# Scores of the two later layers as one fp32r product over 96 stacked rows, with q turned inside the Fourier part

## The chip, the cores and the metric

The program runs on one core of one Trainium2 chip. The time is device microseconds of one execution, as the median of several runs. The engines are named as in the profile: PE is TensorE (PEld its weight loads), DVE is VectorE, ACT is ScalarE, POOL is GpSimd and SP is SyncE, which issues the DMAs.

## What is computed

The reference runs a first block (sparse attention, retention, a gated branch mix and a feed-forward part) and then a second block of two layers on x of 256 tokens by 1024 features. The change touches the second block alone, in both layers, and there the attention's scores:

```
u = rmsnorm(x) @ w_in[l]                 # q, k, v (512 wide each), glu_in, four_in
q = apply_partial_rope(rmsnorm(q, qnorm_g[l]), cos, sin)      # 8 heads x 2 halves x 32
k = apply_partial_rope(rmsnorm(k, knorm_g[l]), cos, sin)
sc = einsum('bqhcd,bkhcd->bhcqk', q, k) * 32 ** -0.5          # two score maps a head
p = softmax(sc);  w = p[:, :, 0] - lam * p[:, :, 1];  att = w @ v
g = ga * sigmoid(gb); cv = depthwise conv of g over 31 taps   # branch b
fr = real(fft2(four_in groups))                               # branch c
x = x + (gates of att, cv, fr branches) @ w_out[l];  x = x + feed-forward(x)
```

## The kernel before

All arithmetic is in 32 bits. A large product is made of three fp32r products: a value is split into an upper part (a copy rounded to fp32r) and a lower part (value less upper part), and upper by upper, lower by upper and upper by lower are added in PSUM. The weights come from memory in 207 chunks of at most 128 x 2048, in the order in which they are used. For every chunk SP issues a load into one of four `raw` buffers (`load_raw`, line 400), ACT writes the upper part `whi` (line 917), and DVE and POOL share the lower part `wlo` (lines 1572 and 1352). SP loads chunk i only when both parts of chunk i - 4 are written (lines 402 and 403), and its queue is strictly in order.

A later layer starts with v, four gated units (glu), then k (`k{l}`), q (`q{l}`) and the Fourier input (`xf{l}`), each as two chunks. `qk_out` normalizes and rotates q and k on DVE, ACT and POOL into `qn`. PE turns them (`qk_turned`, line 796, four 128 x 128 transposes for each half of the tokens) into PSUM, and ACT copies them out as `k2T` and `q2T` in f32 (line 1235). A bank of PSUM that held a turned tile is free for the next use when its last reader has signalled.

Then three stages run as one sequence, `weave(chain(fourier(), attention(), after_attention()), back, 4)`. `back` holds the products of twelve gate units (`g{l}_f`, one chunk and 48 products each) and of the first output projection. `fourier` has five steps with nothing between them. `attention` has 20 steps, with four eighths of a gate unit (24 products) between two of them, so that one chunk is used in two steps. Step u works like this, with u = 2 * head + half of the tokens, for u below 16:

- PE: the two score products of step u (line 861, `scores2`), after the turned weights `W2T` of u - 2 and, in even steps, the product with v.
- DVE: `combine(u - 1)` (reciprocal, factor, one tap of the convolution, then `W2`, line 2078), one tap, then the maximum over the scores of u (line 2100), two taps. The 31-tap convolution is 124 DVE instructions (line 2024) that `conv_some` spreads over the stages, until none is left.
- ACT: the two exponentials `E2` of u (line 1297), every second step a gate's output (line 1250), and after the odd steps the next chunk's `whi`.

DVE has a fixed order too: in the rows of q two taps at each of eight points, in those of xf three, six in each Fourier step. `lower` (line 1605) is the subtraction that makes a lower part, `upper` (line 966) the ACT copy that makes an upper part.

Of the kernel before, what the change touches and what calls it, by code (L numbers as in the profile page):

```python
# [92 lines left out]
for _name, _w in SMALL:  # L93
# [6 lines left out]
    "pool_lo", "pool_small", "d_raw0", "d_raw1", "d_raw2", "d_raw3", "d_x0", "d_x1", "d_small", "d_small2", "d_gain",  # L100
    "d_dec", "d_ctab", "d_gnw", "d_gf", "d_cs", "d_cd", "d_out",
)
# [163 lines left out]
def place(nc, ctx):  # L266
# [79 lines left out]
    z = p + 48  # L346
    t.q2T = at("q2T", z, [128, 4, S])
    t.k2T = at("k2T", z + 4, [128, 4, S])
    t.v2 = [at(f"v2{i}", z + 8 + 2 * i, [128, 512]) for i in range(2)]
# [41 lines left out]
def sp_program(sp, t, ev, d):  # L391
# [5 lines left out]
    def load(sem, dst, src, *names):  # L397
        sp.op.dma_start(dst, src).then_inc(*at(sem, *names, by=16))
# [14 lines left out]
    for i in range(len(PLAN)):  # L413
# [19 lines left out]
        for l in range(2):  # L433
            if i == UNITS[f"k{l}"][0] + 2:
                sp.wait_ge(*on("v ends", l, "pe"))
                sp.wait_ge(*on("v ends", l, "dve"))
                load("d_cs", t.csT[:, :, :], d["in_cs"], ("cs", l))
                load("d_cd", t.cdT[:, :, :], d["in_cd"], ("cd", l))
        load_raw(i)
    for tt in range(2):  # L440
# [6 lines left out]
def pe_program(pe, t, ev, pb):  # L447
# [340 lines left out]
    def layer(l, norm):  # L788
# [13 lines left out]
        run(rows(f"xf{l}", *h))  # L802
        qk_turned("q")
        ev.name("pe_turned", ("projected", l, "pe"))

        def fourier():
            for g in range(5):
                if g < 4:
                    for tt in range(2):
# [18 lines left out]
        def attention():  # L828
            yield
            for u in range(20):  # L830
# [22 lines left out]
                if u < 16:  # L853
                    hd, tt = u // 2, u % 2
                    rg = slice((hd % 4) * 32, (hd % 4) * 32 + 32)
                    for w in "qk":
                        for half_ in range(2):
                            pe.wait_ge(*on("free", (w, l, "T", half_)))
                    pe.wait_ge(*on("E2", l, u - 2) if u >= 2 else on("T12", l, 2 + u))
                    for c in range(2):  # L860
                        product(t.sc[u % 2][:, c * S:c * S + S], t.q2T[rg, c * 2 + hd // 4, tok(tt)],
                                t.k2T[rg, c * 2 + hd // 4, :], names=[("scores2", l, u)] * c)
                yield
# [35 lines left out]
def act_program(act, t, ev, pb):  # L899
# [308 lines left out]
    def layer(l, norm):  # L1208
# [24 lines left out]
        def qk_turned(w):  # L1233
            for tt in range(2):
                turned_out((w, l, "T", tt), (t.q2T if w == "q" else t.k2T)[:, :, tok(tt)])

# [4 lines left out]
                                     [("k", l, "T", tt) for tt in range(2)])))  # L1241
        qk_turned("q")
        done = []

        def gate_out(f):
            def out(p):
                name = (f"g{l}_{f}", 0)
                act.wait_ge(*on("got", *name))
                for v in range(2):
                    act.op.activation(t.gm2[:, 2 * f + v, :], bank(name)[:, v * S:v * S + S],  # L1250
# [15 lines left out]
        def fourier():  # L1266
            for g in range(5):
                if g < 4:
                    act.wait_ge(*on("fourier 1", l, g))
# [278 lines left out]
def dve_program(dve, t, ev, pb):  # L1548
# [438 lines left out]
    def layer(l, norm):  # L1987
# [59 lines left out]
        for w in "kq":  # L2047
            for _ in rows(f"{w}{l}", qk_out(w)):
                conv_some(2)
        for _ in rows(f"xf{l}", value_out(f"xf{l}", t.xf[0][:, :], [("k", l, "T", tt) for tt in range(2)])):  # L2050
            conv_some(3)

        def fourier():
            for g in range(5):
                if g >= 1:
                    k = g - 1
                    lower([("fr", l, k)], t.frl[:, k, :], t.ob[:, 0:256], t.frh[:, k, :], ("fr hi", l, k))
                conv_some(6)
                yield 0
# [225 lines left out]
```

## Time and profile before

| what | value |
|---|---|
| median of three runs | 1472.41 us (1471.64 to 1473.39) |
| the profiled execution | 1471.79 us, span 1470.5 us |
| mean granted TensorE clock | 0.971 |
| PE busy | 1363.5 us, 93% of the span |
| DVE, POOL, ACT busy | 903.7, 733.3, 653.8 us |
| Fourier part and attention of layer 0 | about 585 to 704 us from the span's start |
| the same of layer 1 | about 1066 to 1186 us |

The span starts with the first instruction and ends with the last; 1.3 us of the profiled execution's own time lie around it. The busy share of PE is a mean over stages that have different limits. Times in the rows further down are microseconds from the span's start, and durations without a unit are in microseconds.

### The profile page before, as it was taken

The numbers are of one execution on the slowest core, as the hardware profiler recorded it, in microseconds if no ns is written. First come the engines' busy times: TensorE is split into PE (matmuls) and PEld (weight loads), VectorE is DVE, ScalarE is ACT, GpSimd is POOL, SyncE is SP. The second block draws the span as 40 slices with busy tenths as digits, with TensorE's granted clock in tenths as the row PEclk, the third lists the DMA queues.
The fourth block names the chain that finished last, engine by engine and source line by source line (L and its number), as shares of the span: only waits on it lengthen the run. The fifth ranks groups of instructions, "written<-read, shape, count | busy, mean of one in ns | idle before, by whom it ended". The sixth has DMA issues, their size and how long they took to land. (4 is left out here: it accounts for less than half of the span.)

```text
span 1470.5 us, 21695 instructions
## 1 busy us (share of the span) xinstructions
PE 1363.5 (93%) x8946; PEld 1230.8 (84%) x8946; DVE 903.7 (61%) x1155; ACT 653.8 (44%) x884; POOL 733.3 (50%) x325
## 2 busy tenths in 40 slices
PE   6999999989989898799988999999878999899999
PEld 4878899889978696578987999879657899699987
DVE  5554465467773559976565656445997646556542
ACT  4634435355553443345644444335334464444432
POOL 3653254655554359333665445445833356445453
PEclk9999999999999999999998999999898999899999
DMA  7653224444444452222444455546322234355551
GB/s 276 244 193 144 86 102 172 172 173 172 172 172 172 157 217 88 89 94 104 144 143 158 174 189 182 194 163 219 115 86 87 90 140 147 142 189 182 176 197 58
DMA packets 32786, 227.04 MB, mean 154 GB/s; under 512 B 3632, under 2 KB 4016, under 8 KB 6448
## 3 DMA queue, kind: packets, MB, share of 16 engines
q1 hardware_dynamic: 32688, 225.66, 42.9%
q8 instruction: 71, 1.16, 0.3%
q14 instruction: 27, 0.22, 0.0%
HBM read 224.60 MB, written 1.05 MB: 153 GB/s over the span
## 5 line engine op out<-in xcount | busy, mean ns | idle before, releaser
L1352 POOL TENSOR_TENSOR wlo<-raw,whi 128x416 fp32r<-128x416 f32 (+5 forms) x207 | 604.4, 2923 | 641.2 <-ACT whi L917 543.2
L1572 DVE TENSOR_TENSOR wlo<-raw,whi 128x1632 fp32r<-128x1632 f32 (+5 forms) x207 | 354.5, 1713 | 327.7 <-ACT whi L917 262.2
L519 PE MATMUL ps<-hhi,whi 128*128 128x256 f32 x1696 | 494.5, 292 | 2.6 <-DVE hlo L1605 2.4
L520 PE MATMUL ps<-hlo,whi 128*128 128x256 f32 x1696 | 487.2, 287 | 0.0
L521 PE MATMUL ps<-hhi,wlo 128*128 128x256 f32 x1696 | 486.8, 287 | 0.0
L917 ACT ACTIVATE whi<-raw 128x2048 fp32r<-128x2048 f32 (+1 forms) x207 | 392.6, 1901 | 179.2 <-PE ps L466 153.7
L519 PEld LDWEIGHTS ps<-hhi,whi 128*128 128x128 f32 x1696 | 331.6, 196 | 16.1 <-issue 15.6
L520 PEld LDWEIGHTS ps<-hlo,whi 128*128 128x128 f32 x1696 | 332.0, 196 | 0.4 <-issue 0.2
L521 PEld LDWEIGHTS ps<-hhi,wlo 128*128 128x128 f32 x1696 | 331.7, 196 | 0.0
L2024 DVE SCALAR_TENSOR_TENSOR cv<-gp,sm,cv 128x256 f32<-128x256 f32 x240 | 149.2, 671 | 0.0
L464 PE MATMUL ps<-whi,hhi 128*128 128x512 f32 (+1 forms) x272 | 111.4, 410 | 12.9 <-DVE hlo L1605 5.7
L464 PE MATMUL ps<-whi,ghi 128*128 128x512 f32 x264 | 104.1, 394 | 6.7 <-DVE fu L1951 6.6
L465 PE MATMUL ps<-wlo,hhi 128*128 128x512 f32 (+1 forms) x272 | 107.6, 396 | 0.0
L466 PE MATMUL ps<-whi,hlo 128*128 128x512 f32 (+1 forms) x272 | 107.4, 395 | 0.0
L465 PE MATMUL ps<-wlo,ghi 128*128 128x512 f32 x264 | 103.5, 392 | 0.0
L466 PE MATMUL ps<-whi,glo 128*128 128x512 f32 x264 | 103.5, 392 | 0.0
L1605 DVE TENSOR_TENSOR glo<-fg,ghi 128x256 fp32r<-128x256 f32 x66 | 81.5, 1234 | 2.4 <-ACT ghi L966 2.4
L1171 ACT ACTIVATE fs<-ps 128x256 f32<-128x256 f32 x44 | 16.9, 384 | 147.6 <-PE ps L521 147.6
L1297 ACT ACTIVATE E<-ps,st 128x256 f32<-128x256 f32 x64 | 29.7, 469 | 102.2 <-DVE st L2100 102.2
L464 PEld LDWEIGHTS ps<-whi,hhi 128*128 128x128 f32 x272 | 53.3, 196 | 26.0 <-issue 10.3
L1384 POOL TENSOR_TENSOR st<-st,sm 128x1 f32<-128x1 f32 (+2 forms) x30 | 47.0, 1565 | 50.6 <-DVE st L1624 40.1
L464 PEld LDWEIGHTS ps<-whi,ghi 128*128 128x128 f32 x264 | 50.1, 190 | 17.9 <-DVE fu L1951 7.5
(263 smaller groups left out, 1853.4 us busy)
## 6 DMA issues: line engine op xcount, KB each, us to landing
raw<-in_w SPq DMA_DIRECT2D x205, 1024.0 KB, 4.8
gain<-in_rows SPq DMA_DIRECT2D x6, 512.0 KB, 4.5
raw<-in_w SPq DMA_DIRECT2D x2, 560.0 KB, 5.6
x<-in_x SPq DMA_DIRECT2D x2, 512.0 KB, 6.7
csT<-in_cs SPq DMA_DIRECT2D x2, 512.0 KB, 5.8
out<-x SPq DMA_DIRECT2D x2, 512.0 KB, 2.6
dec<-in_dec SPq DMA_DIRECT2D x1, 768.0 KB, 7.9
sm<-in_small SPq DMA_DIRECT2D x1, 764.0 KB, 15.2
```

The lines of the kernel that those rows point to most:

```text
L464: pe.op.matmul(o, sh, mh, start=start, stop=False, skip_group_check=True)
L465: pe.op.matmul(o, sh, ml, start=False, stop=False, skip_group_check=True)
L466: signalled(pe.op.matmul(o, sl, mh, start=False, stop=stop, skip_group_check=True), names)
L519: pe.op.matmul(o, wh[:, k, c:c + 128], hi[:, k, :], start=first, stop=False, skip_group_check=True)
L520: pe.op.matmul(o, wh[:, k, c:c + 128], lo[:, k, :], start=False, stop=False, skip_group_check=True)
L521: ins = pe.op.matmul(o, wl[:, k, c:c + 128], hi[:, k, :], start=False, stop=last, skip_group_check=True)
L917: act.op.activation(t.whi[i % NHL][:, 0:n], t.raw[i % NRAW][:, 0:n], ACT.Copy).then_inc(*at("act_hi", ("hi", i)))
L1352: pool.op.tensor_tensor(t.wlo[i % NHL][:, c], t.raw[i % NRAW][:, c], t.whi[i % NHL][:, c].bitcast(F32), ALU.subtract).then_inc(*at("pool_l ...
L1384: pool.op.tensor_tensor(o, a, small(t, "mhalf")[:, 0:a.shape[-1]], ALU.pow).then_inc(*at("pool_small", name))
L1572: dve.op.tensor_tensor(t.wlo[i % NHL][:, c], t.raw[i % NRAW][:, c], t.whi[i % NHL][:, c].bitcast(F32), ALU.subtract).then_inc(*at("dve_lo" ...
L1605: dve.op.tensor_tensor(dst, src, hi.bitcast(F32), ALU.subtract).then_inc(*at(sem, *names))
L2024: ins = dve.op.scalar_tensor_tensor(t.cv[:, f, :], t.gp[:, f, j:j + S], cw[:, f, j:j + 1], t.cv[:, f, :], ALU.mult, ALU.add)
```

## The change

The score products of the two later layers are no longer f32 products over 32 rows. k and q are split into upper and lower parts (`kh`, `kl`, `qh`, `ql`). DMAs inside SBUF stack them over 96 partitions: `kst` holds kh, kh, kl, and `qst` holds qh, ql, qh, so that one fp32r product over 96 rows gives the three partial products at once. `qst` has room for four of the eight heads (c * 2 + g for g = 0 or 1); the second group is stacked when the scores of step 7 are done, into the same buffer. A stack is made by 12 DMAs, each from 32 partitions to 32 partitions: 128 KB each for k, 64 KB each for a group of q. All are issued by SP, at a fixed place among the chunk loads. q is turned in the third Fourier step instead of before the first. On DVE, `qk_lower` makes the lower parts, that of k behind the rows of q, with three taps of the convolution drawn ahead of it.

```
@@ sp_program, before load_raw(i)
+            stacked = UNITS[f"xf{l}"][0]
+            if i == stacked + 5:
+                for tt in range(2):
+                    sp.wait_ge(*on("free", ("k", l, "T", tt)))
+                for r, src in enumerate((t.kh, t.kh, t.kl)):
+                    for b in range(4):
+                        load("d_stack", t.kst[32 * r:32 * r + 32, b, :, :].bitcast(F32),
+                             src[32 * b:32 * b + 32, :, :].bitcast(F32),
+                             *([("k stack", l)] * (r + b == 5)))
+            for g, first in enumerate((stacked + 7, stacked + 13)):
+                if i == first:
+                    sp.wait_ge(*on("k stack", l) if g == 0 else on("scores2", l, 7))
+                    for tt in range(2):
+                        sp.wait_ge(*on("free", ("q", l, "T", tt)))
+                    for r, src in enumerate((t.qh, t.ql, t.qh)):
+                        for b in range(4):
+                            load("d_stack", t.qst[32 * r:32 * r + 32, b, :, :].bitcast(F32),
+                                 src[32 * b:32 * b + 32, g:4:2, :].bitcast(F32),
+                                 *([("q stack", l, g)] * (r + b == 5)))
@@ pe_program, layer
         qk_turned("k")
         run(rows(f"xf{l}", *h))
-        qk_turned("q")
@@ fourier, on PE and on ACT
             for g in range(5):
+                if g == 2:
+                    qk_turned("q")
@@ attention, on PE
-                    rg = slice((hd % 4) * 32, (hd % 4) * 32 + 32)
-                    for w in "qk":
-                        for half_ in range(2):
-                            pe.wait_ge(*on("free", (w, l, "T", half_)))
+                    pe.wait_ge(*on("k stack", l))
+                    pe.wait_ge(*on("q stack", l, hd // 4))
...
-                        product(t.sc[u % 2][:, c * S:c * S + S], t.q2T[rg, c * 2 + hd // 4, tok(tt)],
-                                t.k2T[rg, c * 2 + hd // 4, :], names=[("scores2", l, u)] * c)
+                        product(t.sc[u % 2][:, c * S:c * S + S], t.qst[0:96, hd % 4, c, tok(tt)],
+                                t.kst[0:96, hd % 4, c * 2 + hd // 4, :], names=[("scores2", l, u)] * c)
@@ act_program, layer (and gate units 4 to 7 wait for the second q stack)
-                turned_out((w, l, "T", tt), (t.q2T if w == "q" else t.k2T)[:, :, tok(tt)])
+                name = (w, l, "T", tt)
+                upper(("T hi", w, l, tt), (t.qh if w == "q" else t.kh)[:, :, tok(tt)],
+                      bank(name)[:, :].rearrange("p (k s) -> p k s", k=4), name)
@@ dve_program, layer
+        conv_some(3)
+        qk_lower("k")
         for _ in rows(f"xf{l}", ...):
             conv_some(3)
@@ fourier, on DVE
                     k = g - 1
+                    if k == 2:
+                        qk_lower("q")
                     lower([("fr", l, k)], t.frl[:, k, :], t.ob[:, 0:256], t.frh[:, k, :], ("fr hi", l, k))
```

On SP in layer 0, where the chunks of the gate units are loaded, this stands in a row before (one chunk a row, a buffer's number behind raw):

```order
L398 DMA raw_49<-in_w 128x2048 [waits pool_lo,dve_lo]
L398 DMA raw_50<-in_w 128x2048 [waits pool_lo,dve_lo]
L398 DMA raw_51<-in_w 128x2048 [waits pool_lo,dve_lo]
L398 DMA raw_52<-in_w 128x2048 [waits pool_lo,dve_lo]
L398 DMA raw_49<-in_w 128x2048 [waits pool_lo,dve_lo]
L398 DMA raw_50<-in_w 128x2048 [waits pool_lo,dve_lo]
```

and this now, from the second load ahead of the second q stack to the load behind it:

```order
L401 DMA raw_51<-in_w 128x2048 [waits pool_lo,dve_lo]
L401 DMA raw_52<-in_w 128x2048 [waits pool_lo,dve_lo]
L401 DMA qst<-qh 32x2x256 [waits pe_small]
L401 DMA qst<-qh 32x2x256 x3
L401 DMA qst<-ql 32x2x256 x4
L401 DMA qst<-qh 32x2x256 x4
L401 DMA raw_49<-in_w 128x2048 [waits pool_lo,dve_lo]
```

The twelve stacking DMAs of the second group stand right behind the load of chunk xf + 12, which waits for both lower parts of chunk xf + 8.

On DVE in layer 0, from the end of q's rows to the first Fourier lower part, before:

```order
L2043 TENSOR_SCALAR st<-st 128x16 [waits dve_small]
L2024 SCALAR_TENSOR_TENSOR cv<-gp,sm,cv 128x256 x2
L1572 TENSOR_TENSOR wlo_57<-raw_50,whi_54 128x608 [waits pe_weights,act_hi,d_raw1]
L2024 SCALAR_TENSOR_TENSOR cv<-gp,sm,cv 128x256 x2
L2024 SCALAR_TENSOR_TENSOR cv<-gp,sm,cv 128x256 [waits dve_small] x10
L1572 TENSOR_TENSOR wlo_58<-raw_51,whi_55 128x608 [waits pe_weights,act_hi,d_raw2]
L2024 SCALAR_TENSOR_TENSOR cv<-gp,sm,cv 128x256 [waits dve_small] x3
L1610 COPY xf_146<-ps 128x512 [waits pe_turned,pe_weights]
L2024 SCALAR_TENSOR_TENSOR cv<-gp,sm,cv 128x256 [waits dve_small] x15
L1605 TENSOR_TENSOR frl<-ps,frh 128x256 [waits act_small]
```

and now:

```order
L2068 TENSOR_SCALAR st<-st 128x16 [waits dve_small]
L2049 SCALAR_TENSOR_TENSOR cv<-gp,sm,cv 128x256 x4
L2049 SCALAR_TENSOR_TENSOR cv<-gp,sm,cv 128x256 [waits dve_small]
L1630 TENSOR_TENSOR kl<-ps,kh 128x4x128 [waits act_small] x2
L1597 TENSOR_TENSOR wlo_57<-raw_50,whi_54 128x608 [waits pe_weights,act_hi,d_raw1]
L2049 SCALAR_TENSOR_TENSOR cv<-gp,sm,cv 128x256 [waits dve_small] x12
L1597 TENSOR_TENSOR wlo_58<-raw_51,whi_55 128x608 [waits pe_weights,act_hi,d_raw2]
L2049 SCALAR_TENSOR_TENSOR cv<-gp,sm,cv 128x256 [waits dve_small] x3
L1635 COPY xf_150<-ps 128x512 [waits pe_turned,pe_weights]
L2049 SCALAR_TENSOR_TENSOR cv<-gp,sm,cv 128x256 [waits dve_small] x15
L1630 TENSOR_TENSOR frl<-ps,frh 128x256 [waits act_small]
```

Three taps and two subtractions of 128 x 512 now stand ahead of the copy of xf, which the first Fourier product waits for.

On PE in layer 0, the Fourier part now has q's eight transposes behind its first product with `cdT`; before, they stood ahead of the first product with `csT`:

```order
L491 MATMUL ps<-T_152,cdT 128x256 [waits d_cd,act_out]
L491 MATMUL ps<-T_152,cdT 128x256
L499 MATMUL ps<-sm,qn_145 128x128 [waits pool_small]
L499 MATMUL ps<-sm,qn_145 128x128 x3
L499 MATMUL ps<-sm,qn_146 128x128 [waits pool_small]
L499 MATMUL ps<-sm,qn_146 128x128 x3
L491 MATMUL ps<-csT,xf_150 128x512
```

## Rows read from the trace of the kernel before

**Rows 1.** The page, busy time, share of the span and instructions of each engine.

```profile
PE 1363.5 (93%) x8946; PEld 1230.8 (84%) x8946; DVE 903.7 (61%) x1155; ACT 653.8 (44%) x884; POOL 733.3 (50%) x325
```

**Rows 2.** Waits, 585 to 730 us: who waited for whom, total, times, longest.

```profile
ACT E L1297 <- DVE st L2100: 50.8, 16, 5.7
...
PE ps L838 <- DVE W L2078: 11.7, 7, 3.9
...
PE ps L469 <- DVE frl L1605: 5.9, 2, 4.9
```

**Rows 3.** DVE in order of time: start, duration, instruction [idle before].

```profile
631.36 0.79 DVE L1572 TENSOR_TENSOR wlo<-raw,whi 128x608 fp32r<-128x608 f32 x1 [2.15 <-issue]
...
632.45 3.09 DVE L2024 SCALAR_TENSOR_TENSOR cv<-gp,sm,cv 128x256 f32<-128x256 f32 x1
...
639.60 0.69 DVE L2100 TENSOR_REDUCE st<-ps 128x2 f32<-128x512 f32 x1
...
643.23 0.79 DVE L1572 TENSOR_TENSOR wlo<-raw,whi 128x608 fp32r<-128x608 f32 x1 [2.15 <-issue]
```

**Rows 4.** ACT in order of time, the end of the same round.

```profile
640.32 0.47 ACT L1297 ACTIVATE E<-ps,st 128x256 f32<-128x256 f32 x1 [1.11 <-DVE st L2100]
...
641.23 1.90 ACT L917 ACTIVATE whi<-raw 128x2048 fp32r<-128x2048 f32 x1
```

**Rows 5.** PE in order of time: scores, gate products, turned weights.

```profile
607.47 1.13 PE L469 MATMUL ps<-k2T,q2T 32*128 32x256 f32 x4
...
608.75 0.28 PE L520 MATMUL ps<-hlo,whi 128*128 128x256 f32 x1
608.87 0.28 PE L521 MATMUL ps<-hhi,wlo 128*128 128x256 f32 x1
...
647.89 0.44 PE L838 MATMUL ps<-sm,W 128*128 128x128 f32 x2 [1.41 <-DVE W L2078]
...
653.45 1.13 PE L469 MATMUL ps<-k2T,q2T 32*128 32x256 f32 x4
```

**Rows 6.** POOL in order of time: lower parts at the Fourier part and attention.

```profile
584.66 6.61 POOL L1352 TENSOR_TENSOR wlo<-raw,whi 128x1440 fp32r<-128x1440 f32 x2
...
655.16 3.87 POOL L1352 TENSOR_TENSOR wlo<-raw,whi 128x1440 fp32r<-128x1440 f32 x1 [8.01 <-ACT whi L917]
```

**Rows 7.** DVE in order of time, from xf's copy to the Fourier part.

```profile
584.31 0.68 DVE L1610 COPY xf<-ps 128x512 f32<-128x512 f32 x1
584.91 3.28 DVE L2024 SCALAR_TENSOR_TENSOR cv<-gp,sm,cv 128x256 f32<-128x256 f32 x1
...
596.96 2.45 DVE L2024 SCALAR_TENSOR_TENSOR cv<-gp,sm,cv 128x256 f32<-128x256 f32 x6
```

**Rows 8.** DVE, groups by line and form over the span: busy, mean ns.

```profile
L1605 DVE TENSOR_TENSOR hlo<-ps,hhi 128x512 fp32r<-128x512 f32 x24 | 15.9, 688 | 8.4 <-ACT hhi L966 8.3
```

**Rows 9.** SP's queue in order of time: start, time at the issue, what is issued.

```profile
522.14 0.38 SPq L398 DMA_DIRECT2D csT<-in_cs  x1
522.58 0.42 SPq L398 DMA_DIRECT2D cdT<-in_cd  x1
...
659.12 0.33 SPq L398 DMA_DIRECT2D raw<-in_w  x1
```

**Rows 10.** The page, DMA issues: KB each, median us from issue to landing.

```profile
raw<-in_w SPq DMA_DIRECT2D x205, 1024.0 KB, 4.8
...
out<-x SPq DMA_DIRECT2D x2, 512.0 KB, 2.6
```

**Rows 11.** DVE's maxima of steps 0, 8 and 9.

```profile
612.56 0.68 DVE L2100 TENSOR_REDUCE st<-ps 128x2 f32<-128x512 f32 x1
...
660.03 0.68 DVE L2100 TENSOR_REDUCE st<-ps 128x2 f32<-128x512 f32 x1
...
663.38 0.68 DVE L2100 TENSOR_REDUCE st<-ps 128x2 f32<-128x512 f32 x1
```

**Rows 12.** Busy time in one stretch: PE, PEld, DVE, ACT, POOL, granted clock, DMA.

```profile
624.50:631.50 7.00, 7.00 (x29) 6.16 (x29) 4.52 (x12) 5.05 (x12) 0.10 (x1) 0.51 0.37 142
```

More of the change, by code:

```diff
@@ L100 @@
     "pool_lo", "pool_small", "d_raw0", "d_raw1", "d_raw2", "d_raw3", "d_x0", "d_x1", "d_small", "d_small2", "d_gain",
-    "d_dec", "d_ctab", "d_gnw", "d_gf", "d_cs", "d_cd", "d_out",
+    "d_dec", "d_ctab", "d_gnw", "d_gf", "d_cs", "d_cd",
+    "d_stack", "d_out",
 )
@@ L346, in place @@
     z = p + 48
-    t.q2T = at("q2T", z, [128, 4, S])
-    t.k2T = at("k2T", z + 4, [128, 4, S])
+    t.kh, t.kl = (at(n, z + a, [128, 4, S], R32) for n, a in (("kh", 0), ("kl", 4)))
+    t.qh, t.ql = (at(n, p + a, [128, 4, S], R32) for n, a in (("qh", 32), ("ql", 36)))
+    t.kst = at("kst", p, [128, 4, 4, S], R32)
+    t.qst = at("qst", z, [128, 4, 2, S], R32)
     t.v2 = [at(f"v2{i}", z + 8 + 2 * i, [128, 512]) for i in range(2)]
@@ L802, in layer @@
         run(rows(f"xf{l}", *h))
-        qk_turned("q")
-        ev.name("pe_turned", ("projected", l, "pe"))
         def fourier():
             for g in range(5):
+                if g == 2:
+                    qk_turned("q")
                 if g < 4:
@@ L1241, in layer @@
                                      [("k", l, "T", tt) for tt in range(2)])))
-        qk_turned("q")
         done = []
@@ L1248, in out @@
                 act.wait_ge(*on("got", *name))
+                if 4 <= f < 8:
+                    act.wait_ge(*on("q stack", l, 1))
                 for v in range(2):
@@ L1267, in fourier @@
             for g in range(5):
+                if g == 2:
+                    qk_turned("q")
                 if g < 4:
@@ L2049, in layer, with qk_lower @@
                 conv_some(2)
+        def qk_lower(w):
+            for tt in range(2):
+                name = (w, l, "T", tt)
+                hi, lo = (t.qh, t.ql) if w == "q" else (t.kh, t.kl)
+                lower([("free", name)], lo[:, :, tok(tt)], bank(name)[:, :].rearrange("p (k s) -> p k s", k=4),
+                      hi[:, :, tok(tt)], ("T hi", w, l, tt))
+        conv_some(3)
+        qk_lower("k")
         for _ in rows(f"xf{l}", value_out(f"xf{l}", t.xf[0][:, :], [("k", l, "T", tt) for tt in range(2)])):
```

## The prediction

> **What bounds the kernel now.** The page's busy times come first: PE is busy for 1363.5 us, 93% of the span [rows 1]. Read alone, that says that any PE work taken out is time won. The share is a mean, though, so I went to the stretch that the change touches, the Fourier part and the attention of a later layer (585 to 704 us in layer 0; layer 1 repeats it), and asked who waits for whom. PE waits for DVE's `W2` seven times there, 11.7 us in total and 3.9 us at the longest, and 5.9 us for the Fourier lower parts; ACT waits for DVE's maxima in all 16 steps, 50.8 us [rows 2]. So PE is not the engine that sets the pace.
>
> Next, what does? I followed one round of two steps in DVE's order of time. DVE's share of a chunk's lower part starts at 631.36, the next chunk's at 643.23 [rows 3]: a round is 11.87 us. Its links are: DVE's lower part and two small instructions; one tap of the convolution that takes 3.09 us, where six of them take 2.45 us elsewhere [rows 3, 7]; `W2`, tap, maximum; ACT's exponentials; DVE's combine and the odd step's maximum at 639.60 [rows 3]; ACT's exponentials from 640.32; ACT's `whi` of the next chunk at 641.23 for 1.90 us [rows 4]; and at 643.23 DVE again. No link is a PE instruction. PE comes in only if scores are late for a maximum, and they aren't: the scores of step 8 stand from 653.45 [rows 5], their maximum is taken at 660.03 [rows 11].
>
> The long tap lies within a POOL lower part like that of 3.87 us [rows 6]: the tap reads two tensors in SBUF. The Trainium skill has a rule for it (SBUF — State Buffer, "SBUF: two separate sides"): a DVE instruction with two SBUF inputs and a GpSimd instruction exclude each other for a whole instruction. By that rule the new lower parts, which read PSUM and one SBUF tile, would not be held; only the taps ahead of them would be, and by that rule the sum below is as it stands.
>
> **What the change takes off PE.** A step's two score products are four instructions now, 1.13 us from 607.47 [rows 5]. As two fp32r products at the pitch of the gate products (0.12 us from 608.75 to 608.87, same row) they take about 0.3 us. That is 0.8 us a step, 13 us a layer, 26 us in all. I book it at zero: in steps 0 to 15 PE would reach the turning of `W2` 0.8 us sooner and wait 0.8 us longer, since `W2` comes out of a round that has no PE in it (PE's wait of 1.41 us at 647.89 [rows 5] becomes about 3). The cover is gone only if a round gets shorter than PE's own work in it, and nothing in the change shortens it. From the last `W2` on PE sets the end, but there are no scores left there.
>
> **What it adds on DVE ahead of the first scores.** Two k and two q lower parts of 128 x 512, 0.69 us each by the same instruction from PSUM [rows 8], 2.8 us; and three taps drawn ahead (0.41 us each, 2.45 / 6 [rows 7]), 1.2 us that attention gets back later. DVE has no idle time to hide them between q and the attention. Placed on the trace: k's part and the three taps put xf's copy, at 584.31 [rows 7], behind the start of POOL's pair of lower parts (584.66 to 591.27 [rows 6]). The taps ahead of the copy are then held as the one at 584.91 was (3.28 us [rows 7]), twice. I put the copy at 591.5, and the first Fourier product with it, 6 us later than now. Of this DVE's own line only loses about 2.2 us (the 2.5 us of work less an idle of 0.6 us), since the 15 taps behind the copy no longer meet POOL; but PE has then stood for 7 us and restarts at half clock (the granted clock was 0.51 at 624.50 to 631.50, after PE's wait of 3.9 us [rows 2, 12]), and the Fourier steps, a relay of PE, ACT and DVE, lose another 0.8 us by it. q's lower parts, in the fourth step, would end at about 606.5.
>
> Then comes the first q stack: 12 DMAs, one issue after the other. Consecutive issues stand 0.44 us apart (522.14 and 522.58 [rows 9]), so 5.3 us for twelve. The nearest landing is 2.6 us for 512 KB; a load of 1 MB takes 4.8 us [rows 10]. I take 2.6 for the last 64 KB. The scores of step 0 can start at 614.4, and their maximum stands at about 615.5 where it is at 612.56 now [rows 11]: 3 us late. PE has waited for the stack too; its next 24 gate products run at half clock (5 us for 2.9), so step 1's scores come another 1 us late. **Sum: 4 us a layer.** Bounds: 2.5 us, if DVE's 2.8 us less its idle time is all; 7 us, if the landing is 4.8 us and the half clock lasts through. k's stack is covered: it can start when k's lower parts are done, about 578, and has 36 us. q's eight transposes move into PE's wait for the Fourier lower parts.
>
> **What it adds on SP: the second q stack.** Its 12 DMAs stand right behind the load of chunk xf + 12, which waits for POOL's lower part of chunk xf + 8. That part starts at 655.16 and takes 3.87 us [rows 6]; the load goes out at 659.12 [rows 9], though step 7's scores follow the turning at 647.89 [rows 5], some 10 us before. Step 8 needs this stack. From 659.12: the load's own issue 0.4 us, twelve issues of 0.44 us, landing 2.6 us: 667.4. Scores 0.4 us, maximum at 667.9 instead of 660.03 [rows 11], 7.9 us late. Queued behind the waiting scores on PE are 24 gate products, the turning of step 7's `W2` and the scores of step 9. PE has stood for more than 10 us, so these run at half clock: 5.1 us for the 24, and step 9's maximum comes some 6 us behind step 8's, where it is 3.35 us now (660.03 and 663.38 [rows 11]); 2.7 us more. **Sum: 10.6 us a layer.** Bounds: 6.5 us (issues 0.33 us apart, as the busy time of one is, landing 2.6 us, half of the clock loss); 13.5 us (landing as a 1 MB load's, 4.8 us, and all of it).
>
> The Trainium skill speaks against this form of transfer (DMA: Bandwidth & Descriptors, "Rules for kernel authors"): many small transfers should be coalesced, under 64 KB they are mostly overhead. It gives about 2.0 us of fixed cost for a DMA on another queue; with it in place of the landing of 2.6 us each stack would be 0.5 us sooner.
>
> **What it adds later.** After the last `W2` PE runs without waits, and a PE that stood longer before it may restart at half clock: 0 to 2 us, I take 0.5. ACT's copies only change their form, and its new wait for the second stack comes eight steps after the stack. The waits of SP delay loads that are used 12 us later or more.
>
> **Sum.** 4 + 10.6 + 0.5 = 15 us a layer, 30 us in two. The profiled execution took 1471.8 us, 0.6 us under the median of the three runs. 1471.8 + 30 = 1502 us.
>
> **Rivals.**
> 1. PE is the bound after all, and its 26 us come back: 1446 us. For it: 93% busy. Against it: the W2 waits, and a round without PE. It decides if the score products stood between a maximum and the `W2` before it; it would show as rounds of less than 11.87 us. With the additions of the first part it would still be some 1455 us. Chance 6%.
> 2. The second stack is hidden or nearly so, and only the lead-in costs: 8 to 12 us, 1482 us. It asks that the stack goes out some 8 us before POOL's lower part ends, or that twelve issues and the landing take under 2 us. Against it: the order on SP. Chance 10%.
> 3. The DMAs within SBUF are slower than loads: each reads 32 partitions and writes 32, and no DMA in the trace does that. If they take 1 us each one after the other, each stack is 6 to 7 us later: 13 us more a layer, 1528 us. Chance 13%.
> 4. Everything cancels within 0.2% (about 3 us): 3%, as a meeting of 1 and 3.
>
> The forecast, both terms within their bounds, has 68%. Its bounds are 9 x 2 = 18 us and 22.5 x 2 = 45 us, 1490 to 1517 us. To hold the time 8 times in 10 I widen it to 1486 to 1520 us, into the near parts of rivals 2 and 3. Faster by over 0.2% (what a measurement of this kernel can tell from no change): 6%. Within: 3%. Slower: 91%.
>
> **What would show it.** On PE, a wait for the stack DMAs ahead of step 0's scores and one of about 10 us or more ahead of step 8's, in both layers, with a granted clock near 0.5 behind it. On DVE, maxima of steps 0, 8 and 9 late by about 3, 12 and 15 us in layer 0, and rounds of 11.9 us in between, unchanged. PE busy down by 20 us or so, W2 waits up. On SP, the twelve issues 0.44 us apart, right behind a load. The prediction is wrong in its base if the rounds get shorter, and in its size if the last small DMA lands much later or sooner than 2.6 us after its issue.

## The result, and the profile after

| | before | after |
|---|---|---|
| time, us, median (lowest to highest) | 1472.9 (1471.6 to 1477.4) | 1512.0 (1507.8 to 1513.7) |
| profiled execution, us | 1471.8 | 1507.8 |
| ratio, 95% interval | | 1.0256 [1.0225, 1.0286] |

The change makes the kernel 39 us slower. The forecast was 1502 us in a range of 1486 to 1520: the sign and the main mechanism held, and 9 of the 39 us were missing. The profiled execution is the fastest of after, 4 us under the median, so 36 of the 39 us (1507.8 less 1471.8) can be found in the trace.

The page, busy time, share of the span and instructions of each engine, answering to [rows 1]:

```profile
PE 1345.3 (89%) x8882; PEld 1227.9 (82%) x8882; DVE 910.5 (60%) x1163; ACT 654.5 (43%) x884; POOL 729.3 (48%) x325
```

PE does 18 us less and DVE 7 us more. Who waited for whom (total, times, longest) from 570 to 760 us, answering to [rows 2]:

```profile
ACT E L1322 <- DVE st L2136: 58.0, 14, 15.1
...
PE ps L491 <- DMA qst<-qh: 19.5, 2, 14.5
PE ps L860 <- DVE W L2114: 16.7, 7, 4.0
```

PE's waits for `W2` went up from 11.7 (the same from 570 to 760 us) to 16.7 us, and two waits for the q stack are new, 4.9 and 14.5 us. PE in order of time, at the scores of steps 0 and 8 and behind the latter [rows 5]:

```profile
615.83 0.77 PE L491 MATMUL ps<-kst,qst 96*128 96x256 f32 x2 [4.91 <-DMA qst<-qh]
...
673.89 0.80 PE L491 MATMUL ps<-kst,qst 96*128 96x256 f32 x2 [14.54 <-DMA qst<-qh]
674.48 0.41 PE L541 MATMUL ps<-hhi,whi 128*128 128x256 f32 x1
674.70 0.41 PE L542 MATMUL ps<-hlo,whi 128*128 128x256 f32 x1
...
678.05 0.28 PE L543 MATMUL ps<-hhi,wlo 128*128 128x256 f32 x1
678.17 0.29 PE L541 MATMUL ps<-hhi,whi 128*128 128x256 f32 x1
```

The gate products behind the stall start 0.22 us apart, and 0.12 us apart from 678.05 on: PE restarts at half its clock. The mean granted clock from 674 to 681 us was 0.72:

```profile
674.00:681.00 7.00, 7.00 (x44) 7.00 (x45) 3.09 (x7) 2.92 (x10) 0.00 (x0) 0.72 0.00 0
```

DVE in order of time [rows 3, 7, 11]: the taps ahead of xf's copy, the copy, the maxima of steps 0 and 1, two maxima that stand a round apart, and those of steps 8 and 9.

```profile
577.42 12.08 DVE L2049 SCALAR_TENSOR_TENSOR cv<-gp,sm,cv 128x256 f32<-128x256 f32 x12
...
591.31 0.68 DVE L1635 COPY xf<-ps 128x512 f32<-128x512 f32 x1
...
616.64 0.69 DVE L2136 TENSOR_REDUCE st<-ps 128x2 f32<-128x512 f32 x1 [0.69 <-PE ps L491]
...
621.26 0.69 DVE L2136 TENSOR_REDUCE st<-ps 128x2 f32<-128x512 f32 x1 [1.18 <-PE ps L491]
...
629.81 0.68 DVE L2136 TENSOR_REDUCE st<-ps 128x2 f32<-128x512 f32 x1
...
641.68 0.68 DVE L2136 TENSOR_REDUCE st<-ps 128x2 f32<-128x512 f32 x1
...
674.72 0.69 DVE L2136 TENSOR_REDUCE st<-ps 128x2 f32<-128x512 f32 x1 [9.30 <-PE ps L491]
...
679.56 0.69 DVE L2136 TENSOR_REDUCE st<-ps 128x2 f32<-128x512 f32 x1 [2.06 <-PE ps L491]
```

A round is 11.87 us, as before (641.68 less 629.81). SP's queue [rows 9], first the first q stack, then the second, and POOL's lower part that the load ahead of the second one waits for [rows 6]:

```profile
606.59 2.60 SPq L401 DMA_DIRECT2D qst<-qh  x4
609.23 2.51 SPq L401 DMA_DIRECT2D qst<-ql  x4
611.78 2.51 SPq L401 DMA_DIRECT2D qst<-qh  x4
...
664.80 2.52 SPq L401 DMA_DIRECT2D qst<-qh  x4
```

```profile
660.52 3.82 POOL L1377 TENSOR_TENSOR wlo<-raw,whi 128x1440 fp32r<-128x1440 f32 x1 [8.01 <-ACT whi L937]
```

Four issues take 2.5 us and the next four start 2.6 us later. From the first issue to the scores it is 9.2 us at the first stack (606.59 to 615.83) and 9.1 at the second (664.80 to 673.89). The page, DMA issues [rows 10] (KB each, median us to landing):

```profile
kst<-kh SPq DMA_DIRECT2D x16, 128.0 KB, 2.4
qst<-qh SPq DMA_DIRECT2D x32, 64.0 KB, 2.0
```

Executions differ by some us before they reach the place that the change touches, so I measure each from ACT's copy of the turned k, the last thing that all have alike:

```profile
569.30 1.08 ACT L986 ACTIVATE kh<-ps 128x512 fp32r<-128x512 f32 x2
```

In the kernel before it starts at 570.52. From there to the maximum of step 0 it is 42.0 us before and 47.3 after in layer 0, and 42.0 and 48.0 in layer 1; from that maximum to the one of step 15 it is 82.8 us before and 94.9 after in layer 0, and 83.5 and 93.3 in layer 1. Of the 94.9 us, the second stack's stall accounts for 10.8: step 8's maximum is 17.9 us behind step 7's (656.86) where it was 8.5, and step 9's 4.8 us behind step 8's where it was 3.35.

### The profile page after: what moved, and what is told of

It is laid out like the page before. It is cut to its first block and busy times, and to the rows that moved or that the text cites. A ratio compares the mean times of both kernels' runs of the same rounds, so it can differ in the third digit from the quotient of the medians.

```text
span 1506.5 us, 21651 instructions
## 1 busy us (share of the span) xinstructions
PE 1345.3 (89%) x8882; PEld 1227.9 (82%) x8882; DVE 910.5 (60%) x1163; ACT 654.5 (43%) x884; POOL 729.3 (48%) x325
## 5 line engine op out<-in xcount | busy, mean ns | idle before, releaser
L541 PEld LDWEIGHTS ps<-hhi,whi 128*128 128x128 f32 x1696 | 337.3, 199 | 4.4 <-issue 4.1
L542 PEld LDWEIGHTS ps<-hlo,whi 128*128 128x128 f32 x1696 | 337.3, 199 | 0.5 <-issue 0.2
L543 PEld LDWEIGHTS ps<-hhi,wlo 128*128 128x128 f32 x1696 | 336.5, 198 | 0.0
L486 PEld LDWEIGHTS ps<-whi,hhi 128*128 128x128 f32 x272 | 53.4, 196 | 26.2 <-issue 10.4
L1409 POOL TENSOR_TENSOR st<-st,sm 128x1 f32<-128x1 f32 (+2 forms) x30 | 46.6, 1554 | 50.9 <-DVE st L1649 40.3
```

Of the source, the lines that this page charges most:

```text
L486: pe.op.matmul(o, sh, mh, start=start, stop=False, skip_group_check=True)
L541: pe.op.matmul(o, wh[:, k, c:c + 128], hi[:, k, :], start=first, stop=False, skip_group_check=True)
L542: pe.op.matmul(o, wh[:, k, c:c + 128], lo[:, k, :], start=False, stop=False, skip_group_check=True)
L543: ins = pe.op.matmul(o, wl[:, k, c:c + 128], hi[:, k, :], start=False, stop=last, skip_group_check=True)
L1409: pool.op.tensor_tensor(o, a, small(t, "mhalf")[:, 0:a.shape[-1]], ALU.pow).then_inc(*at("pool_small", name))
```

## Experiments

The kernels were timed in three groups, each on its own chip beside the kernel before: A, B, C and G (before: 1474.9 us), D, E, H and I (1474.7), F, J, K and L (1473.4). A ratio goes by the kernel before of its own group. In the table "lead-in" is the time from ACT's copy of the turned k to step 0's maximum in layer 0, and "steps" that from step 0's maximum to step 15's in layer 0 / layer 1.

| kernel | median us | ratio [95%] | lead-in | steps |
|---|---|---|---|---|
| before | 1472.9 | | 42.0 | 82.8 / 83.5 |
| after | 1512.0 | 1.0256 [1.0225, 1.0286] | 47.3 | 94.9 / 93.3 |
| A, fp32r alone | 1473.7 | 0.9991 [0.998, 1.0002] | 42.6 | 82.7 / 83.4 |
| B, no stacks | 1485.9 | 1.0073 [1.0058, 1.0088] | 47.5 | 82.2 / 82.2 |
| C, second stack earlier | 1492.2 | 1.0117 [1.0096, 1.0137] | 47.4 | 84.6 / 82.9 |
| D, C and DVE's old order | 1489.7 | 1.0112 [1.0092, 1.0132] | 47.4 | 85.0 / 83.8 |
| E, D and q turned first | 1486.6 | 1.0103 [1.007, 1.0135] | 48.0 | 83.4 / 82.9 |
| F, E and k's lower parts at the copy | 1480.1 | 1.0043 [1.0027, 1.0059] | 44.5 | 83.7 / 83.7 |
| G, before with POOL's share cut | 1443.2 | 0.9781 [0.9757, 0.9806] | 36.9 | 74.4 / 74.7 |
| H, G and A | 1442.2 | 0.9793 [0.9767, 0.9818] | 36.9 | 74.4 / 74.8 |
| I, E and POOL's share cut | 1464.7 | 0.9927 [0.9902, 0.9953] | 43.6 | 77.4 / 76.8 |
| J, G and `whi` ahead | 1429.1 | 0.9692 [0.9669, 0.9715] | 36.8 | 67.5 / 67.5 |
| K, J and A | 1415.9 | 0.960 [0.9579, 0.962] | 36.9 | 60.6 / 61.0 |
| L, F, share cut, `whi` ahead | 1434.9 | 0.9734 [0.970, 0.9767] | 40.3 | 68.4 / 67.9 |

### A. PE's saving alone

The turned q and k are rounded to fp32r, so each score is one product over 32 rows. The lower parts are left out of the scores: it computes less, and shows a worth, not a kernel.

```
-    t.q2T = at("q2T", z, [128, 4, S])
-    t.k2T = at("k2T", z + 4, [128, 4, S])
+    t.q2T = at("q2T", z, [128, 4, S], R32)
+    t.k2T = at("k2T", z + 4, [128, 4, S], R32)
```

> The kernel before, with q2T and k2T rounded to fp32r, so that a step's two score products take one fp32r pass each over 32 rows; the lower parts of q and k are left out of the scores, and nothing is added on DVE or SP. It gives PE the whole saving of the change (some 0.8 us a step, 26 us) and none of its costs. Theory 1 (the pace of the attention is a round of DVE, ACT and POOL without PE): the same time as before, 1472 us, within 4 us; rounds of 11.9 us, PE's waits for W2 up by 10 us or more a layer. Theory 2 (PE is the bound): 1446 to 1452 us, rounds shorter than 11.9 us.

Measured: 1473.7 us, ratio 0.9991 [0.998, 1.0002], so theory 1 held. The scores' two products fell from 1.13 to 0.50 us in the trace, 10 us over 16 steps, and PE waits 7.9 us longer for `W2` (585 to 730 us; 11.7 us before):

```profile
PE ps L838 <- DVE W L2078: 19.6, 9, 4.6
```

So in this kernel PE's saving is worth 3 us at the most by the interval, and nothing that can be told from zero.

### B. The change without its stacks

The 72 DMAs, their waits and the two buffers are left out; the order of all else is that of after. What stands in place of the one product (with g = hd // 4):

```
+    o, j = t.sc[u % 2][:, c * S:c * S + S], c * 2 + hd // 4
+    product(o, t.qh[rg, j, tok(tt)], t.kh[rg, j, :], True, False)
+    product(o, t.ql[rg, j, tok(tt)], t.kh[rg, j, :], False, False)
+    product(o, t.qh[rg, j, tok(tt)], t.kl[rg, j, :], False, True, ...)
```

> The changed kernel without its 72 stacking DMAs: the scores are three fp32r products over 32 rows each, read from qh, ql, kh and kl directly; the order on DVE, ACT and PE stays, with q turned inside the Fourier part. Theory 1 (the two waits for q's stacks make up most of the loss, the rest is DVE's added work ahead of xf's copy and in the Fourier part): 1481 us, 1478 to 1486; maxima of step 0 some 4 us later than in the kernel before, no loss at step 8. Theory 2 (the loss is DVE's work and the later q): 1500 us or more.

Measured: 1485.9 us, within what was expected. So 26 of the 39 us are the stacks and 13 (11 against the kernel before of its own group) are the lower parts and their order. The scores of B are three products where after has one, but PE has time for them: the steps are no longer than before. The lead-in is the surprise: without any stack it is 47.5 us, 5.5 more than before where some 4 were expected, and no shorter than with the stacks. DVE in order of time, the last Fourier lower part to step 0's maximum:

```profile
612.57 0.42 DVE L1615 TENSOR_TENSOR frl<-ps,frh 128x256 fp32r<-128x256 f32 x1 [0.27 <-ACT frh L971]
612.91 5.52 DVE L2034 SCALAR_TENSOR_TENSOR cv<-gp,sm,cv 128x256 f32<-128x256 f32 x6
618.36 0.78 DVE L1582 TENSOR_TENSOR wlo<-raw,whi 128x608 fp32r<-128x608 f32 x1
619.06 0.47 DVE L2034 SCALAR_TENSOR_TENSOR cv<-gp,sm,cv 128x256 f32<-128x256 f32 x1
619.46 0.68 DVE L2121 TENSOR_REDUCE st<-ps 128x2 f32<-128x512 f32 x1
```

DVE is busy up to the maximum and waits for no scores: its own line is late, and in after the first stack arrives at the same time. The stack costs step 1 another 1.3 us there (621.26 is 4.6 us behind step 0's maximum, against 3.3 here), in layer 0 alone: in layer 1 it is 3.3 us in both.

### C. The second stack one load earlier on SP

```
-            for g, first in enumerate((stacked + 7, stacked + 13)):
+            for g, first in enumerate((stacked + 7, stacked + 12)):
```

> The changed kernel with one number changed: the second q stack stands ahead of the load of chunk xf + 12 instead of behind it, so that it waits for step 7's scores and no longer for POOL's lower part of chunk xf + 8. The same 12 DMAs at the same pace. Theory 1 (the place on SP's queue costs 10.8 us a layer): the stack starts about 11 us earlier and lands ahead of need, 1490 us, 1487 to 1495. Theory 2 (issue and landing, about 9.5 us together, are what step 8 waits for, wherever they stand): a wait of several us is left at step 8, 1500 us or more.

Measured: 1492.2 us, 20 us less than after: theory 1 held. DVE, the maxima of steps 8 and 9:

```profile
668.94 0.68 DVE L2136 TENSOR_REDUCE st<-ps 128x2 f32<-128x512 f32 x1
...
672.75 0.69 DVE L2136 TENSOR_REDUCE st<-ps 128x2 f32<-128x512 f32 x1 [1.04 <-PE ps L491]
```

Step 8 is 8.5 us behind step 7 again, and step 9 loses 0.5 us. Half of the change's price was this one place in SP's queue, behind a load that waited for POOL.

### D and E. DVE's order given back, q turned first

D is C with the three taps no longer drawn ahead and `qk_lower("k")` behind the rows of xf. E is D with q turned ahead of the Fourier part and `qk_lower("q")` right behind `qk_lower("k")`:

```
-        conv_some(3)
-        qk_lower("k")
         for _ in rows(f"xf{l}", ...):
             conv_some(3)
+        qk_lower("k")
+        qk_lower("q")      # E only
```

> The changed kernel with its second q stack at the earlier place (the run before measured 1492.2 us, ratio 1.0117 to the kernel before, and both layers' attention began 5.3 us late), and with VectorE's order of the kernel before given back in one place: no three taps drawn ahead, and k's lower parts behind the copy of xf. Theory 1 (VectorE's queue ahead of the Fourier part makes the lead-in late: the copy of xf stands behind three taps of 1.27 us together and behind k's lower parts, 1.27 us, and behind what these push it past): step 0 comes 2.5 to 4 us earlier in each layer, 1485 us, 1482 to 1488, ratio 1.005 to 1.009. Theory 2 (the lead-in is the chain of q's turn, lower parts and stack, which ends at the wait for the stack): step 0 moves by under 1 us a layer, 1491 us.

> As the run above, and q is turned ahead of the Fourier part on TensorE and ScalarE as in the kernel before, its lower parts right behind k's on VectorE. Theory 1: what then stays of the change per layer is 2.5 us of lower parts on VectorE and about 1.5 us at step 9, so 1480 us, 1476 to 1484, ratio 1.002 to 1.007. Theory 2 (the twelve issues at 0.64 us and the landing behind them set the start whatever the order): no gain on the run above. The stack's chain should end at least 8 us ahead of step 0, so that no wait for it is left there.

Both expectations failed: 1489.7 us where 1482 to 1488 was expected, and 1486.6 where 1476 to 1484 was; the lead-in is 47.4 and 48.0 us. The copy of xf did come early (14.0 and 13.8 us behind the turned k; 13.8 before, 22.0 after), so theory 1 was right on what delayed the copy and wrong that this decides. The two are late for different reasons.

In D it is theory 2: DVE's line got shorter and then stood for the stack. PE's scores, DVE's maximum of step 0, and the landing of the first q stack (595 to 620 us):

```profile
618.96 0.77 PE L491 MATMUL ps<-kst,qst 96*128 96x256 f32 x2 [6.47 <-DMA qst<-qh]
```

```profile
619.77 0.69 DVE L2135 TENSOR_REDUCE st<-ps 128x2 f32<-128x512 f32 x1 [3.33 <-PE ps L491]
```

```profile
qst<-qh SPq DMA_DIRECT2D x8, 64.0 KB, 5.2
```

Without its wait of 3.33 us DVE would have taken the maximum 44.1 us behind the turned k. But k's lower parts ended at 597.6, the k stack was issued from 597.63 to 605.90, and the q stack, which waits for it, from 607.65. Two 1 MB loads had gone out in between, at 606.00; the landings were 5.2 us instead of the 2.0 of after's first stack, and from the first issue to the scores it took 11.3 us instead of 9.2.

In E, where q comes first, the maximum waits for no scores. Of E, DVE and PE in order of time:

```profile
584.60 9.39 DVE L2047 SCALAR_TENSOR_TENSOR cv<-gp,sm,cv 128x256 f32<-128x256 f32 x9
593.91 1.28 DVE L1628 TENSOR_TENSOR kl<-ps,kh 128x512 fp32r<-128x512 f32 x2
```

```profile
594.64 1.97 PE L499 MATMUL ps<-sm,qn 128*128 128x128 f32 x8 [9.69 <-DVE kl L1628]
```

The stack was not 8 us early, as expected, either: its DMAs landed after 5.4 to 5.5 us (median, again behind two loads) and PE could start the scores at 616.65, 1.6 us ahead of the maximum. PE can't turn q before k's lower parts have read the PSUM banks that hold the turned k. An early place for them delays the copy of xf; a late one lies behind taps that POOL's pair holds, and delays the turning of q and, PE's work being in order, the whole Fourier part.

### F. k's lower parts directly behind the copy

```
+        def xf_then_k(tt):
+            xf_out(tt)
+            if tt == 0:
+                qk_lower("k")
+        for _ in rows(f"xf{l}", xf_then_k):
             conv_some(3)
-        qk_lower("k")
         qk_lower("q")
```

> The run with q turned first, and one group of VectorE moved: k's lower parts stand directly behind the copy of xf, ahead of the nine taps that GpSimd's pair holds. Theory 1 (both of these lead-ins were late by a PSUM bank: q's turn needs the banks that k's lower parts still read, and these stood behind held taps, 9.7 us of TensorE's time): TensorE turns q at once, step 0 comes 42.5 to 44.5 us after k's turn instead of 48.0 (42.0 in the kernel before), in both layers, and the time is 1478 us, 1475 to 1482, ratio 1.001 to 1.005. Theory 2 (the twelve issues at 0.64 us and the landing behind them set the lead-in, wherever the lower parts stand): step 0 stays at 46 us or more, 1485 us or more, ratio 1.007 or above.

Measured: 1480.1 us, ratio 1.0043 [1.0027, 1.0059]; the lead-in is 44.5 us, and 42.6 in layer 1. Theory 1 held. DVE, PE and POOL in order of time:

```profile
588.62 0.68 DVE L1633 COPY xf<-ps 128x512 f32<-128x512 f32 x1
589.22 1.27 DVE L1628 TENSOR_TENSOR kl<-ps,kh 128x512 fp32r<-128x512 f32 x2
590.42 8.25 DVE L2047 SCALAR_TENSOR_TENSOR cv<-gp,sm,cv 128x256 f32<-128x256 f32 x9
```

```profile
589.95 1.25 PE L499 MATMUL ps<-sm,qn 128*128 128x128 f32 x8 [0.27 <-DVE kl L1628]
```

```profile
588.98 6.63 POOL L1375 TENSOR_TENSOR wlo<-raw,whi 128x1440 fp32r<-128x1440 f32 x2
```

The wait of 9.7 us is 0.3 us. What stays in layer 0 is 2.5 us of lead-in, as much as the four lower parts take on DVE, and 0.9 us at step 9; in layer 1 it is 0.5 us (42.6 against 42.0) and 0.2 us in the steps. The trace has 1.8 and 2.4 us more behind step 15 of the two layers than before; their cause was not looked for. Nothing is left out here, and PE does what the change wanted; it is 6.7 us slower than before. I did not find an order in which it is faster than before while the rounds are as long as they are.

### G and H. A shorter round

G is the kernel before, with POOL left 128 of the 2048 columns of a gate chunk's lower part; H is G with the edit of A, so it leaves the lower parts out of the scores too.

```
-SHARES = (... (85, 0.3), ... (152, 0.3), ...)
+SHARES = (... (85, 0.95), ... (152, 0.95), ...)
```

> The kernel before with DVE's share of the lower parts of the gate chunks at 0.95 instead of 0.3, in both layers; POOL keeps 128 of 2048 columns. In a round DVE then works 1.3 us longer on a chunk, and its tap or W2 is no longer held for 2.6 us by POOL. Theory 1 (the round of 11.9 us is DVE's and includes the held tap): rounds 1.2 us shorter until PE's own work of 9.7 us in a round is met; some 8 us a layer and 3 us more in the lead-in, 1450 to 1462 us. Theory 2 (DVE is short of time, and any work given to it costs): slower than before, 1480 us or more.

> Two edits to the kernel before: q and k turned are written as fp32r and the scores are one fp32r product over the same 32 rows (the lower parts of q and k are left out of the scores: less is computed), and GpSimd's share of the weight lower parts in the later layers is cut as in the run that took 1443.2 us (ratio 0.9781). In that run TensorE streams without a gap through the rounds of 10.6 us for two steps. Theory 1 (the bound has passed to TensorE there, so its 0.8 us a step now count): 32 steps by 0.5 to 0.8 us are 16 to 26 us, 1422 us, 1417 to 1428, ratio 0.961 to 0.968. Theory 2 (VectorE's round still sets the pace also at the smaller share): 1443 us, ratio 0.978, as alone the same edit was worth 0.0009.

G took 1443.2 us, below the 1450 to 1462 expected (the lead-in alone is 5.2 us shorter, where 3 were expected), and H 1442.2 us where 1417 to 1428 was: theory 2. G's round is 10.62 us (DVE in order of time, the lower part and what follows it, and POOL):

```profile
639.61 2.16 DVE L1572 TENSOR_TENSOR wlo<-raw,whi 128x1920 fp32r<-128x1920 f32 x1 [2.16 <-issue]
...
642.08 0.47 DVE L2024 SCALAR_TENSOR_TENSOR cv<-gp,sm,cv 128x256 f32<-128x256 f32 x1
```

```profile
639.66 2.43 POOL L1352 TENSOR_TENSOR wlo<-raw,whi 128x128 fp32r<-128x128 f32 x1 [8.19 <-ACT whi L917]
```

The tap behind it takes 0.47 us instead of 3.09 [rows 3]: the hold is gone, at the price of 1.4 us of DVE's own work. The expectation of H went wrong at a reading. I had taken G's gapless PE between 632 and 644 us for a bound. It was PE catching up after a stretch at a lower clock (0.68 from 625 to 632 us):

```profile
625.00:632.00 7.00, 7.00 (x38) 6.54 (x38) 4.81 (x10) 2.82 (x5) 2.43 (x1) 0.68 0.00 1
```

From 632 to 644 us the granted clock was 1.00, and PE's turnings of `W2` stand 9.52 us apart for two steps,

```profile
634.41 0.38 PE L838 MATMUL ps<-sm,W 128*128 128x128 f32 x2
...
643.93 0.38 PE L838 MATMUL ps<-sm,W 128*128 128x128 f32 x2
```

less than the round of 10.62. PE's work in a round is 9.5 us, not the 10.4 that I put into the expectation of J. In J, where PE has no gap either, the same distance is 9.53 us (636.74 to 646.27).

### I. The changed kernel in the shorter round

E with the SHARES of G.

> The run with q turned first, and GpSimd's share cut as in the run that took 1443.2 us; nothing is left out of the computation. Theory 1 (TensorE is the bound of the short rounds): the stacked scores give back 0.8 us a step, 16 to 26 us of the two layers, against 4 us a layer for lower parts and stacks, 1430 us, 1422 to 1438, ratio 0.966 to 0.975, so it beats both kernels and the run with the share alone. Theory 2 (VectorE sets the short rounds, or the stacks' waits return because the rounds are shorter): 1450 us or more, ratio 0.983 or above.

Measured: 1464.7 us, ratio 0.9927 [0.9902, 0.9953]: faster than before, but 21 us slower than G, which has the old scores. That is theory 2: PE still waits for `W2` (11.7 us in layer 0, 585 to 730 us), so its saving counts for nothing, and it waits 6.9 us for k's lower parts and 8.0 us for the two q stacks. The lead-in is 6.7 and 6.4 us longer than G's and the steps 3.0 and 2.1 us, 18 of the 21 us.

### J, K and L. `whi` ahead of the exponentials

In G's round DVE still stands 2.16 us in front of its lower part (the row at 639.61), while ACT makes the upper part behind the exponentials. J moves it ahead of those of the odd steps; K is J with the edit of A; L is F with J's two edits, the whole change in a short round.

```
@@ attention, on ACT
+                if u < 16 and u % 2:
+                    splits(upto[0])
                 if u < 16:
```

> The kernel before with GpSimd's share cut (1443.2 us alone) and one move on ScalarE: the upper part of the weights of the next gate chunk (1.9 us) stands ahead of the exponentials of the odd steps instead of behind them. Theory 1 (the round of 10.6 us is a chain that VectorE and ScalarE share: maximum, exponentials, upper part of the weights, VectorE's lower part, which waits 2.2 us for it): the wait of 2.2 us goes, and the round falls until TensorE is the bound; TensorE's own work is 10.4 us of the 10.6, so 16 rounds by 0.2 us, 1440 us, 1436 to 1443, ratio 0.974 to 0.978. Theory 2 (the exponentials are late instead, by 0.8 us in each odd step, and nothing is gained or something is lost): 1443 us or more.

> The same two edits with the scores as one fp32r product over 32 rows (the lower parts of q and k are left out of the scores: less is computed). With the share alone this was 1442.2 us, ratio 0.9793. Theory 1 (TensorE's saving counts once the chain of ScalarE and VectorE is shorter than TensorE's work): the round falls to 9.1 to 9.7 us, 16 rounds by 0.9 to 1.5 us, 1424 us, 1416 to 1430, ratio 0.961 to 0.970, and 10 us or more under the run beside it. Theory 2 (TensorE is not the bound there either): within 3 us of the run beside it.

> All together, and nothing is left out of the computation: the stacked scores with q turned first, k's lower parts behind the copy of xf and the second stack at the earlier place, GpSimd's share cut, and the upper part of the weights ahead of the exponentials. Theory 1: the run beside it with one product, and 2 to 4 us a layer for the lower parts, the stack and its wait at step 8, 1431 us, 1422 to 1438, ratio 0.965 to 0.975, under the run with TensorE's old scores. Theory 2 (the stack's wait at step 8 grows as the rounds shorten, and the lead-in stays late): 1445 us or more, above the run with the old scores.

J took 1429.1 us, below the 1436 to 1443 expected; the expectation had read PE's work too large. ACT and DVE of J in order of time:

```profile
638.15 1.92 ACT L917 ACTIVATE whi<-raw 128x2048 fp32r<-128x2048 f32 x1
639.95 0.48 ACT L1299 ACTIVATE E<-ps,st 128x256 f32<-128x256 f32 x1
```

```profile
638.22 0.69 DVE L2102 TENSOR_REDUCE st<-ps 128x2 f32<-128x512 f32 x1 [0.51 <-PE ps L469]
638.82 0.87 DVE L2026 SCALAR_TENSOR_TENSOR cv<-gp,sm,cv 128x256 f32<-128x256 f32 x2
640.16 2.16 DVE L1574 TENSOR_TENSOR wlo<-raw,whi 128x1920 fp32r<-128x1920 f32 x1 [0.46 <-issue]
```

Here, for the first time with the old scores, a maximum of the rounds waits for PE, and PE waits for `W2` no more. Now the saving counts: K is 13.2 us faster than J with nothing else changed, as expected (10 us or more), 0.4 us of the 0.63 us that a step's scores save. Up to step 6 J's rounds are as short as K's, 8.4 to 8.6 us; behind it they are 9.1 to 9.6 us and K's 7.8 to 8.5, and only there is the saving seen. K leaves the lower parts out of the scores, so it shows a worth, not a kernel. L computes everything, and lands at 1434.9 us: 19.0 us above K and 5.8 us above J. It is within the 1422 to 1438 of its theory 1, but not under the run with the old scores, as that had said. The four times of L lie from 1430.3 to 1440.4 us, those of J from 1428.1 to 1429.6, so the order is clear and the size is not. L waits for both stacks (585 to 715 us):

```profile
PE ps L491 <- DMA qst<-qh: 9.7, 2, 5.5
```

Its lead-in is 3.5 us longer than K's (5.2 in layer 1) and its steps 7.7 and 6.9 us. In this order the stacks and lower parts cost more than the product saves, even where PE is the bound. The fastest kernel with nothing left out is J, at 0.969 of before, with the old scores.

## Why the prediction was right, and where it was short

- **PE is not the bound, its saving books at zero: right.** A measures it as 1.2 us, between 3 us saved and none, and after's rounds stayed at 11.87 us. The saving itself was 0.63 to 0.66 us a step, not 0.8 (two stacked products take 0.47 us at full clock, not 0.3); as it was booked at zero this changes nothing. By H it was worth nothing at 10.6 us either, and by J and K it becomes worth something where the round comes down to PE's 9.5 us: the cover that the prediction named (a round shorter than PE's own work) is the one that had to go.
- **xf's copy at 591.5: 591.31, in part by luck.** That execution was 1.2 us ahead at the turned k. Measured from there the copy is at 22.0 us where the forecast meant 21.0 (591.5 less 570.52; 13.8 before). Held taps stand ahead of it, as foreseen: twelve taps in 12.08 us, where twelve free ones take 4.9. The row in F bears out the mechanism with the change's own instruction: k's two lower parts, which read PSUM and one SBUF tile, took 1.27 us within POOL's pair, the taps behind them 8.25 us for nine (3.7 us elsewhere). By the Trainium skill (SBUF — State Buffer, "SBUF: two separate sides") a DVE instruction with two SBUF inputs and a GpSimd instruction that reads SBUF exclude each other, and the trace agrees: the taps were held and the lower parts were not.
- **Lead-in, forecast 3 us at step 0 and 4 with step 1; measured 5.3 and 6.6 in layer 0, 5.9 and 5.9 in layer 1.** Two terms were too small. The failed step is "DVE's own line only loses about 2.2 us" (the terms named with it, 2.5 less 0.6, give 1.9): B shows it lose 5.5 us without a stack. By the rows that is 2.5 us of lower parts, 1.2 us of the three taps drawn ahead (counted as time that attention gets back later, but ahead of step 0 they are still in the way) and some 1.8 us of waits in the Fourier relay (1.55, 0.66 and 0.27 us in B, where before had one of 0.67), for which I had 0.8. The other is the stack itself: its issues stand 0.64 us apart, not 0.44, so twelve take 7.7 us, not 5.3. The landing counts from the start of the last issue, 2.0 us, so that stack and landing took 9.2 us for 7.9. In after both lines end close together: DVE would have been ready 4.6 us late, and the scores made it 5.3. Mending DVE's line does not help while the stack stands, as D showed.
- **Second stack, forecast 10.6 us; measured 10.8 in layer 0.** The place was right: POOL's lower part ends at 664.34 and the stack follows at 664.80. Step 8 was 9.3 us late, not 7.9 (1.2 us more from the first issue to the scores), and the half clock behind it cost 1.5 us, not 2.7: PE was back at full clock by 678.05, 4.2 us after its restart, while I had all 24 products at the slow pace. In layer 1 the steps are 9.8 us longer in all. C gives the whole of this place as 20 us for two layers. From the turned k, the maxima of steps 0, 8 and 9 are 5.3, 15.9 and 17.4 us late in layer 0, where 3, 12 and 15 stood in the forecast.
- **Tail, forecast 0.5 us:** it took 1.3 us in layer 0 (from step 15's maximum to the sum of squares, 22.0 us against 20.7) and 2.8 us in layer 1 (from step 15's maximum to the end). B and F have it too, 0.9 and 2.2 us, and 1.8 and 2.4. What makes it is not shown.
- **The sum.** Layer 0 gives 5.3 + 1.3 (step 1) + 10.8 + 1.3, 18.7 us against 15; layer 1 gives 5.9 + 9.8 (its steps, 93.3 against 83.5 us) + 2.8, 18.5 us. Two layers are 37.2 us; less the 1.2 us by which after was ahead at the turned k, these are the 36 us between the two traces. The other executions of after are 4 us longer than the profiled one; no trace shows where those went.
- **Rival 3** (slower DMAs within SBUF) was a part of the truth, in the issues and not in the landing: 0.64 us for an issue lies between its 1 us and my 0.44. I took the pitch from two loads of 128 partitions, though the rival named the very form that no row showed.
- **k's stack, "covered": right in after, and it hides a risk.** It was issued from 576.87 us. Where k's lower parts come late, as in D, it goes out from 597.63 and the q stack has to wait for it.

Open: I didn't try a second buffer for `qst`, which would take the wait for step 7 off the second stack, nor issues from a second queue.

## What to carry to other kernels

Work taken off the busiest engine was worth nothing here until the chain that sets the pace was shorter than that engine's own work; take that work from the distance of two like instructions in a stretch where the engine never waits and has its full clock, not from its busy share. An instruction that reads a PSUM bank a second time is a release like any other, and its place in the queue decides when that bank's next user may start. A transfer with a date stands on its queue in front of loads whose waits end after that date, and a dozen small ones cost a dozen issues before the first byte of use.

## What the runs showed of the hardware

- **Issues of DMAs within SBUF.** Twelve DMAs from 32 to 32 partitions are issued 0.64 us apart, both at 64 KB and at 128 KB (twelve in 7.6 to 8.3 us in the kernels with stacks), against 0.44 us between two loads [rows 9].
- **Their landing was longer behind loads.** With no load just ahead, the 64 KB DMAs of after's first stack landed 2.0 us after the issue. Behind one 1 MB load (after's second stack) the median was 3.3 to 3.4 us, and behind two (the first stack in layer 0 of D, E, F, I and L) 5.2 to 5.5 us. The Trainium skill (DMA: Bandwidth & Descriptors, "Anatomy of one DMA") gives a fixed cost of about 2.0 us for a DMA issued by GpSimd. These are issued by SP; the undisturbed landings agree with the figure, and those behind loads do not. No run changed the loads alone, so that they are the cause is likely and not shown. In after the pitch of the issues, not the landing, added up.
- **The hold between POOL and DVE works both ways.** In G, POOL's 128 x 128 lower part took 2.43 us, as long as DVE's 2.16 us instruction beside it, although a 128 x 224 one took 0.64 us in E (two in 1.28 us).
- **The clock after a stall.** After standing 14.5 us PE ran 4.2 us at half clock (1.2 GHz), with products 0.22 us apart, and then at full clock (2.4 GHz), with products 0.12 us apart.
